# A SwiGLU's second down projection by 2x2 block products with seven products instead of eight

## The chip, the cores and the metric

One core of a Trainium2 chip. The metric is the device time of one execution in microseconds (us). The kernel before: median 1369.47 us of 3 runs (1368.84 to 1370.0).

## The reference, cut to what matters

Two post-norm layers over 512 tokens with 1024 channels. Layer 0 has a convolution and gating mixer, layer 1 dilated attention; after each mixer stands a SwiGLU with 2816 hidden channels, and after each of the four sublayers a LayerNorm.

```python
def swiglu(x, w_gate, w_up, w_down):
    return (jax.nn.silu(x @ w_gate) * (x @ w_up)) @ w_down

for layer in range(DEPTH):                      # DEPTH = 2
    h = ...                                     # mixer
    x = layer_norm(DN_ALPHA * x + h, ln_g[layer, 0], ln_b[layer, 0])
    x = layer_norm(DN_ALPHA * x + swiglu(x, ffn_w_gate[layer], ffn_w_up[layer], ffn_w_down[layer]),
                   ln_g[layer, 1], ln_b[layer, 1])
```

The change touches `@ w_down` of layer 1: hidden values (512 tokens x 2816) times weights (2816 x 1024). All values are float32.

## The kernel before, in words

**Products in three parts.** Each float32 operand is split into a high part (rounded to float32r) and a low part (the rest). A product is three matmuls: high x high, high x low, low x high (`tokens`, L730 to L736). ScalarE makes the high parts (`split_high`, L1191 to L1201), GpSimd the low parts of weights (`split_low`, L615 to L618), VectorE the low parts of activations (`low_ht`, L2028 to L2032).

**Slabs.** Weights stream in slabs of 128 x 1024 floats (512 KB) through a ring of four: four staging buffers, four high and four low. SP loads slab n when the low part of slab n-4 is done (`load_view`, L513 to L524). ScalarE makes the high part of slab n when TensorE has used slab n-4 (`w_used`). Every engine has one instruction queue that runs in the order written; semaphores join them.

**Up projection.** The gate and up products of 20 of the 22 hidden tiles (units) already use a seven-product scheme whose weight sums VectorE makes in SBUF. The last unit's hidden tile is made by `corner_12` (L2014), ScalarE's `unit_gate` (L1445) and `unit_hidden` (L2020, L2025).

**Second down projection.** It is the last stage before the last norm. Row tile k of the hidden values (128 channels x 512 tokens) is multiplied with slab k: four token tiles x two column halves x three matmuls, 24 matmuls of 128x128 by 128x512 (`whole_rows`, L886). The results of all tiles fill the eight PSUM banks, two banks for each token tile. The last three slabs go token tile by token tile (`finish_tiles`, L900), so that the norm of one tile runs while the next is multiplied. For the hidden tiles ScalarE writes the high part (`high_ht`, L1450 to L1457) and VectorE the low part, into nine slots.

**Last norm.** For each token tile: VectorE adds the residual and sums (`norm_in`, L1664, L1668), ScalarE squares and sums (L1221) and takes the root (L1226), VectorE applies the gain (L1684) and takes the reciprocal (L1689), ScalarE scales into `x_res` (L1234, L1237), GpSimd adds the shift (L626). The last tile ends on VectorE instead (L1680, L1693, L1698).

**Attention.** It takes 72 slabs, in two turns of four heads: first queries and keys, then twelve slabs of values. GpSimd does nothing there but the low parts, in a loop of four. At the end of a turn, behind the values' slabs, ScalarE's queue sends row statistics and factors through device memory (`far_rows`, `far_nat`, `fac_rows`, `fac_far`, and the 1 MB `v_rows`), VectorE weighs the probabilities with them (L2191, L2192), and TensorE transposes them (L1080).

## Time and profile before

| | |
|---|---|
| median of 3 runs | 1369.47 us (1368.84 to 1370.0) |
| profiled execution: span | 1369.0 us, 20672 instructions; no time around it is listed |
| TensorE matmul busy | 1355.4 us, 99% |
| VectorE, ScalarE, GpSimd busy | 887.1 us (65%), 615.3 us (45%), 451.1 us (33%) |
| granted TensorE clock, mean | 0.997 of full speed |
| device memory | 133.56 MB read, 4.24 MB written, 101 GB/s over the span |

Busy time of TensorE counts overlapping matmuls once, so 99% says that it is nearly never without one. In a timeline row stand the start, the duration, engine and line, and in brackets the idle time before it and what ended that; "x2" marks merged instructions. The duration of an instruction includes its fill and drain: the next of the same engine can start a little before its end, so two starts tell the pitch. PE is TensorE, PEld its weight loads, DVE VectorE, ACT ScalarE, POOL GpSimd, SP the queue that issues the loads.

### The profile page before, as it was taken

How to read it: one execution, taken by the hardware profiler on the slowest of the kernel's cores; microseconds unless marked ns; L12 is line 12 of the kernel's file. 1: busy time of each engine (PE TensorE's matmuls, PEld its weight loads, DVE VectorE, ACT ScalarE, POOL GpSimd, SP SyncE). 2: the span in 40 equal slices, each digit the busy share in tenths (PEclk: the TensorE clock that was granted, in tenths of full speed). 3: DMA queues.
4: the chain of work that ended last, by engine and by line, in shares of the span. 5: the costliest groups of instructions: out<-in, count | busy, mean ns of one | idle time of the engine just before them, and what ended most of it. 6: DMA issues, size and time to landing. Idle time of an engine off the chain costs nothing.

```text
span 1369.0 us, 20672 instructions
## 1 busy us (share of the span) xinstructions
PE 1355.4 (99%) x8121; PEld 1208.5 (88%) x8121; DVE 887.1 (65%) x1122; ACT 615.3 (45%) x959; POOL 451.1 (33%) x218
## 2 busy tenths in 40 slices
PE   8999999999999999999999999999999999999997
PEld 7887899999988889888888888888889999998886
DVE  3997698888856355677433665724159888885445
ACT  4465555555542454333433434434255555554233
POOL 4785600000054454344443332444260000005443
PEclk9999999999999999999999999999999999999999
DMA  9323223343453323332442322254122334335321
GB/s 269 93 94 92 63 78 108 92 122 92 112 167 95 105 62 93 93 93 84 132 124 67 88 82 73 77 164 130 47 62 78 107 92 122 92 113 164 96 74 62
DMA packets 181961, 138.72 MB, mean 101 GB/s; under 512 B 8789, under 2 KB 162153, under 8 KB 181896
## 3 DMA queue, kind: packets, MB, share of 16 engines
q1 hardware_dynamic: 175272, 133.52, 33.3%
q10 hardware_dynamic: 6624, 4.29, 1.3%
q8 instruction: 45, 0.74, 0.2%
q14 instruction: 20, 0.16, 0.0%
HBM read 133.56 MB, written 4.24 MB: 101 GB/s over the span
## 4 chain that ended last, share of the span: by engine, by line
PE 97%; DVE 1%; DMA 1%; ACT 1%; SPq 0%; issue 0%; DVEq 0%
PE pq L940 10%; PE pq L939 10%; PE pq L937 10%; PE pq L712 9%; PE pq L714 9%; PE pq L713 9%; PE pq L734 8%; PE pq L735 8%; PE pq L736 8%; PE pq L1130 3%; PE pq L1131 3%; PE pq L1129 3%; PE pq L1108 1%; PE pq L1067 1%; PE pq L1080 1%; PE pq L1101 1%
## 5 line engine op out<-in xcount | busy, mean ns | idle before, releaser
L618 POOL TENSOR_TENSOR w_lo<-stage,w_hi 128x1024 fp32r<-128x1024 f32 x154 | 374.5, 2441 | 873.9 <-ACT w_hi L1201 873.8
L1201 ACT ACTIVATE w_hi<-stage 128x1024 fp32r<-128x1024 f32 x156 | 161.6, 1056 | 238.2 <-PE pq L736 164.8
L712 PE MATMUL pq<-xt_hi,w_hi 128*128 128x512 f32 (+1 forms) x624 | 228.4, 366 | 0.5 <-DVE xt_lo L1653 0.4
L714 PE MATMUL pq<-xt_hi,w_lo 128*128 128x512 f32 (+1 forms) x624 | 225.2, 361 | 0.0
L713 PE MATMUL pq<-xt_lo,w_hi 128*128 128x512 f32 (+1 forms) x624 | 225.1, 361 | 0.0
L940 PE MATMUL pq<-xt_hi,w_lo 128*128 128x256 f32 x632 | 178.9, 283 | 0.0
L939 PE MATMUL pq<-xt_lo,w_hi 128*128 128x256 f32 x632 | 178.9, 283 | 0.0
L937 PE MATMUL pq<-xt_hi,w_hi 128*128 128x256 f32 x632 | 178.8, 283 | 0.0
L712 PEld LDWEIGHTS pq<-xt_hi,w_hi 128*128 128x128 f32 x624 | 117.9, 189 | 19.5 <-DVE xt_lo L1653 1.2
L714 PEld LDWEIGHTS pq<-xt_hi,w_lo 128*128 128x128 f32 x624 | 117.8, 189 | 18.0
L937 PE MATMUL pq<-xs_hi,w_hi 128*128 128x256 f32 x472 | 133.6, 283 | 0.0
L939 PE MATMUL pq<-xs_lo,w_hi 128*128 128x256 f32 x472 | 133.6, 283 | 0.0
L940 PE MATMUL pq<-xs_hi,w_lo 128*128 128x256 f32 x472 | 133.6, 283 | 0.0
L713 PEld LDWEIGHTS pq<-xt_lo,w_hi 128*128 128x128 f32 x624 | 117.9, 189 | 17.1
L937 PEld LDWEIGHTS pq<-xt_hi,w_hi 128*128 128x128 f32 x632 | 121.3, 192 | 0.1
L939 PEld LDWEIGHTS pq<-xt_lo,w_hi 128*128 128x128 f32 x632 | 121.3, 192 | 0.1
L940 PEld LDWEIGHTS pq<-xt_hi,w_lo 128*128 128x128 f32 x632 | 121.3, 192 | 0.0
L2032 DVE TENSOR_TENSOR xs_lo<-ht,xs_hi 128x512 fp32r<-128x512 f32 x26 | 63.4, 2440 | 67.7 <-ACT xs_hi L1457 67.7
L937 PEld LDWEIGHTS pq<-xs_hi,w_hi 128*128 128x128 f32 x472 | 90.6, 192 | 0.0
L939 PEld LDWEIGHTS pq<-xs_lo,w_hi 128*128 128x128 f32 x472 | 90.6, 192 | 0.0
L940 PEld LDWEIGHTS pq<-xs_hi,w_lo 128*128 128x128 f32 x472 | 90.6, 192 | 0.0
L734 PE MATMUL pq<-w_hi,xs_hi 128*128 128x512 f32 x208 | 81.0, 389 | 0.0
(261 smaller groups left out, 2808.4 us busy)
## 6 DMA issues: line engine op xcount, KB each, us to landing
stage<-in_od_w_qkv_dram SPq DMA_DIRECT2D x72, 512.0 KB, 3.9
stage<-in_ffn_w_gate_dram SPq DMA_DIRECT2D x44, 512.0 KB, 4.9
stage<-in_ffn_w_up_dram SPq DMA_DIRECT2D x44, 512.0 KB, 3.9
stage<-in_ffn_w_down_dram SPq DMA_DIRECT2D x44, 512.0 KB, 3.5
stage<-in_ev_w_in_dram SPq DMA_DIRECT2D x16, 512.0 KB, 5.7
stage<-in_ev_w_out_dram SPq DMA_DIRECT2D x8, 512.0 KB, 3.6
stage<-in_od_w_out_dram SPq DMA_DIRECT2D x8, 512.0 KB, 3.9
x_res<-in_x_dram SPq DMA_DIRECT2D x4, 512.0 KB, 6.2
```

The lines of the kernel that those rows point to most:

```text
L618: pool.tensor_tensor(w_lo[slab % RING][:, :], w_stage[slab % RING][:, :], w_hi[slab % RING][:, :].bitcast(F32), ALU.subtract).then_inc(w_l ...
L712: pe.matmul(o, hi[:, k, :], x_hi, start=(k == 0), stop=False)
L713: pe.matmul(o, hi[:, k, :], x_lo, start=False, stop=False)
L714: last = pe.matmul(o, lo[:, k, :], x_hi, start=False, stop=(k == KD - 1))
L734: pe.matmul(o, t_hi[:, tile * P:(tile + 1) * P], hi, start=first, stop=False)
L735: pe.matmul(o, t_hi[:, tile * P:(tile + 1) * P], lo, start=False, stop=False)
L736: return pe.matmul(o, t_lo[:, tile * P:(tile + 1) * P], hi, start=False, stop=end)
L937: pe.matmul(o, hi[:, k, :], x_block[0][:, k, :], start=(first and k == 0), stop=False, skip_group_check=True)
L939: pe.matmul(o, hi[:, k, :], x_block[1][:, k, :], start=False, stop=False, skip_group_check=True)
L940: last = pe.matmul(o, lo[:, k, :], x_block[0][:, k, :], start=False, stop=(k == KH - 1), skip_group_check=True)
L1201: act.activation(w_hi[slab % RING][:, :], w_stage[slab % RING][:, :], ACT.Copy).then_inc(w_hi_ready, 1)
L2032: dve.tensor_tensor(lo, ht[:, k, :], hi.bitcast(F32), ALU.subtract).then_inc(ht_set, 1)
```

## The change: what it does, and the diff

The hidden values H are cut into 2 x 2 blocks for each pair of row tiles (two channel tiles x two halves of 256 tokens), the weights W of the pair into 2 x 2 blocks (two row tiles x two halves of 512 columns). With sums of blocks of H and of W, seven block products for each of the 11 pairs give the result instead of eight; a block product is 6 matmuls.

- **Weight sums.** During attention GpSimd issues six steps per pair (`block_sums`), one behind each low part: three copies and four adding transfers, all from device memory to device memory, into `t_rows`, with three waits for landing per pair. Each pair has two slabs of sums (2 x 512 KB) and a half slab; its seven transfers write 2.5 MB. GpSimd's loop over the attention slabs is written out.
- **39 slabs instead of 22**, numbered here 0 to 38: 0 to 21 are the two sum slabs of each pair, 22 and 23 plain rows of the first two pairs, 24 to 29 the fourth sums (29 is half a slab), 30 to 38 plain rows of the other nine pairs. SP waits for all sums before slab 0.
- **Low parts.** GpSimd makes those of slabs 0 to 3, VectorE those of slabs 4 to 38.
- **Hidden sums.** VectorE forms three sums per pair and later a fourth; ScalarE rounds them, VectorE makes their low parts.
- **Corners.** After the eleventh pair ScalarE copies two token-pairs' results out of PSUM and VectorE combines them in four steps; the rows then accumulate onto the banks.
- **Order at the end.** Token tiles 0 and 1 are complete after slab 29, tiles 2 and 3 after slab 38. The norm of tiles 0 and 1 is interleaved, on ScalarE's and VectorE's queues, with slabs 33, 34 and 35 to 38 (`between`).

```diff
...
-N_SLABS = S_DOWN1 + N_DOWN
+PAIRS = KF // 2
+FRONT_ROWS = 2
+SUM4_SLABS = (PAIRS + 1) // 2
+S_REST = S_DOWN1 + 2 * PAIRS
+S_SUM4 = S_REST + FRONT_ROWS
+S_ROWS = S_SUM4 + SUM4_SLABS
+N_SLABS = S_ROWS + PAIRS - FRONT_ROWS
+OP_SLOTS = 4
...
+            if S_DOWN1 <= slab < S_REST:
+                return t_rows[slab - S_DOWN1].unsqueeze(1)
+            if S_SUM4 <= slab < S_ROWS:
+                return t_rows[2 * PAIRS + slab - S_SUM4][:, 0:slab_width(slab)].unsqueeze(1)
+            if slab >= S_REST:
+                return rows(ffn_w_down[1], 2 * row_pair(slab) + 1)
...
+            def load_down(first, layer, e, end):
+                if layer:
+                    sp.wait_ge(t_four, 16 * PAIRS)
                 load(first)
                 load(first + 1)
                 load_ln(e, layer, 1)
-                for slab in range(first + 2, first + N_DOWN):
+                for slab in range(first + 2, end):
                     load(slab)
...
+            def block_sums(j, step):
+                left, right = slice(0, 512), slice(512, SLAB)
+                upper, lower = (ffn_w_down[1][(2 * j + n) * P:(2 * j + n + 1) * P, :] for n in range(2))
+                both, own = t_rows[2 * j], t_rows[2 * j + 1]
+                four = t_rows[2 * PAIRS + j // 2][:, (j % 2) * 512:(j % 2) * 512 + 512]
+                if step == 0:
+                    pool.dma_start(own, upper).then_inc(t_copied, 16)
+                elif step == 1:
+                    pool.dma_start(both.rearrange("p (a n) -> p a n", a=2),
+                                   lower[:, right].unsqueeze(1).broadcast_to([P, 2, 512])).then_inc(t_copied, 16)
+                    pool.dma_start(four, lower[:, left]).then_inc(t_copied, 16)
+                elif step == 2:
+                    pool.wait_ge(t_copied, 48 * (j + 1))
+                    pool.dma_start(both.rearrange("p (a n) -> p a n", a=2),
+                                   upper[:, right].unsqueeze(1).broadcast_to([P, 2, 512]), accum_op=ALU.add
+                                   ).then_inc(t_two, 16)
+                elif step == 3:
+                    pool.dma_start(own[:, right], upper[:, left], accum_op=ALU.add).then_inc(t_two, 16)
+                elif step == 4:
+                    pool.wait_ge(t_two, 32 * (j + 1))
+                    pool.dma_start(both[:, left], upper[:, left], accum_op=ALU.add).then_inc(t_three, 16)
+                else:
+                    pool.wait_ge(t_three, 16 * (j + 1))
+                    pool.dma_start(four, both[:, left], accum_op=ALU.add).then_inc(t_four, 16)
             feed_forward(S_DOWN0, 1)
-            with pool.Fori(0, N_ATT // RING - 1) as t:
-                for j in range(RING):
-                    split_low(S_ATT + RING + j, t)
+            for n, slab in enumerate(range(S_ATT + RING, S_OUT1)):
+                split_low(slab)
+                if n < 6 * PAIRS:
+                    block_sums(*divmod(n, 6))
             for slab in range(S_OUT1, S_UP1):
                 split_low(slab)
             norm(2, S_UP1)
-            feed_forward(S_DOWN1, 3)
+            for slab in range(S_DOWN1, S_DOWN1 + RING):
+                split_low(slab)
+            norm(3, N_SLABS)
...
+            def down_by_blocks(down, done):
+                def product(slab, side, t_hi, t_lo, part, tile, right, first=False, end=False, resumed=False):
...
+                for j in range(PAIRS):
+                    both, own = down + 2 * j, down + 2 * j + 1
+                    op, first, end = op_pair(j), j == 0, j == PAIRS - 1
+                    def by_three(): return product(both, 0, *op, 2, 0, 1, first, end)
+                    def by_two(): return product(both, 1, *op, 0, 0, 0, first, end)
+                    def by_own(): return product(own, 0, *op, 3, 2, 0, first, end)
+                    def by_own_two(): return product(own, 1, *op, 1, 2, 1, first, end)
+                    slab_ready(both)
+                    pe.wait_ge(op_lo_set, 2 * j + 1)
+                    if not end:
+                        by_three()
+                        by_two().then_inc(w_used, 1)
+                        slab_ready(own)
+                        pe.wait_ge(op_lo_set, 2 * j + 2)
+                        if first:
+                            pe.wait_ge(hid_set, done + KF)
+                        by_own()
+                        by_own_two().then_inc(w_used, 1)
+                        continue
+                    slab_ready(own)
+                    pe.wait_ge(op_lo_set, 2 * j + 2)
+                    by_own()
+                    by_three().then_inc(m_done, 1)
+                    by_own_two().then_inc(m_done, 1)
+                    by_two().then_inc(w_used, 2)
...
+                def plain_rows(slab):
+                    rows_ready(slab)
+                    if slab == S_REST:
+                        pe.wait_ge(corner_set, 1)
+                    op = op_row(slab - S_REST)
+                    product(slab, 0, *op, 1, 2, 0, resumed=True)
+                    if slab == S_REST:
+                        pe.wait_ge(corner_set, 2)
+                    product(slab, 1, *op, 0, 2, 1, resumed=True).then_inc(w_used, 1)
+                for slab in range(S_REST, S_SUM4):
+                    plain_rows(slab)
+                pe.wait_ge(corner_set, 4)
+                for slab in range(S_SUM4, S_ROWS):
+                    rows_ready(slab)
...
+                for slab in range(S_ROWS, N_SLABS - 3):
+                    plain_rows(slab)
+                for slab in range(N_SLABS - 3, N_SLABS):
+                    rows_ready(slab)
+                for r in range(2):
+                    for slab in range(N_SLABS - 3, N_SLABS):
+                        t_hi, t_lo = op_row(slab - S_REST)
+                        for side in range(2):
+                            part = slice((1 - side) * HALF, (2 - side) * HALF)
+                            last = tokens(slab, 512 * side, 512, pq[:, 2 * (2 + r) + side, :], t_hi[:, part], t_lo[:, part],
+                                          r, False, slab == N_SLABS - 1, True)
+                        if r:
+                            last.then_inc(w_used, 1)
+                    if r == 0:
+                        last.then_inc(acc_done, 1)
...
+                def high_sums(j):
+                    act.wait_ge(h_sum_set, 2 * j + 2)
...
+                    act.activation(op_pair(j)[0][:, 0:3 * HALF].rearrange("p (b n) -> p b n", n=HALF), pair_sums(j), ACT.Copy
+                                   ).then_inc(op_hi_set, 1)
+                def high_own(j):
+                    act.wait_ge(hid_set, done + 2 * j + 1)
+                    act.activation(op_pair(j)[0][:, 3 * HALF:4 * HALF], pair_blocks(j)[:, 1, :], ACT.Copy
+                                   ).then_inc(op_hi_set, 1)
+                def high_row(slab):
+                    split_high(slab)
...
+                    act.activation(op_row(m)[0][:, 0:src.shape[1] * HALF].rearrange("p (b n) -> p b n", n=HALF), src, ACT.Copy
+                                   ).then_inc(op_hi_set, 1)
...
                 root(0)
+                if between:
+                    between(0)
                 scale(0)
                 squares_of(1)
                 root(1)
+                if between:
+                    between(1)
                 if e == 3:
                     act.wait_ge(x_scaled, SCALED_PARTS * e + 2)
                     act.wait_ge(ln_loaded[e], 32)
                     act.activation(tile_banks(0), halves(norm_g[:, :]), ACT.Copy).then_inc(gain_copied, 1)
                 scale(1)
+                if between:
+                    between(2)
...
+                if layer:
+                    high_sums(0)
+                    split_high(down + 1)
+                    high_own(0)
+                    unit_gate(last, last % 2)
+                    split_high(down + 2)
+                    split_high(down + 3)
+                    high_sums(1)
+                    high_own(1)
+                    for j in range(2, PAIRS):
+                        split_high(down + 2 * j)
+                        split_high(down + 2 * j + 1)
+                        high_sums(j)
+                        high_own(j)
+                    for slab in range(S_REST, S_SUM4):
+                        high_row(slab)
+                    for n, (dst, bank) in enumerate(((sums, 1), (gate, 5))):
+                        act.wait_ge(m_done, n + 1)
+                        for r in range(2):
+                            last = act.activation(dst[:, r, :], pq[:, bank + 2 * r, :], ACT.Copy)
+                        last.then_inc(m_kept_set, 1)
+                    for slab in range(S_SUM4, S_ROWS + 3):
+                        high_row(slab)
+                    def between(n):
+                        for slab in ((S_ROWS + 3,), (S_ROWS + 4,), range(S_ROWS + 5, N_SLABS))[n]:
+                            high_row(slab)
+                    norm(e, N_SLABS, between)
+                    return
...
+                if e == 3 and i == 1:
+                    dve.wait_ge(w_used, plain(S_ROWS))
+                elif i < TILES - 1:
+                    dve.wait_ge(acc_done, e * (TILES - 1) + i + (e < 3 or i == 0))
                 else:
...
+            def norm(e, between=None):
                 def low(i):
                     if e < 3:
                         x_low(e + 1, i)
                 norm_in(e, 0)
+                if between:
+                    between(0)
                 norm_gain(e, 0)
                 norm_scale(e, 0)
                 norm_in(e, 1)
+                if between:
+                    between(1)
                 norm_gain(e, 1)
                 norm_scale(e, 1)
+                if between:
+                    between(2)
...
+                def low_slab(slab):
+                    width = slab_width(slab)
+                    dve.wait_ge(w_hi_ready, plain(slab) + 1)
+                    dve.wait_ge(w_lo_ready, plain(slab))
+                    dve.tensor_tensor(w_lo[slab % RING][:, 0:width], w_stage[slab % RING][:, 0:width],
+                                      w_hi[slab % RING][:, 0:width].bitcast(F32), ALU.subtract).then_inc(w_lo_ready, 1)
+                def sums_of(j):
+                    blocks, room = pair_blocks(j), pair_sums(j)
+                    dve.wait_ge(hid_set, done + 2 * j + 2)
...
+                    dve.tensor_tensor(room[:, 0:2, :], blocks[:, 1:3, :], blocks[:, 0:1, :].broadcast_to([P, 2, HALF]),
+                                      ALU.subtract).then_inc(h_sum_set, 1)
+                    dve.wait_ge(h_sum_set, 2 * j + 1)
+                    dve.tensor_tensor(room[:, 2, :], room[:, 1, :], blocks[:, 1, :], ALU.add).then_inc(h_sum_set, 1)
+                def fourth_sum(j):
+                    blocks, room = pair_blocks(j), pair_sums(j)
+                    dve.wait_ge(h_sum_set, 2 * j + 2)
+                    dve.tensor_tensor(blocks[:, 0, :], blocks[:, 3, :], room[:, 2, :], ALU.subtract).then_inc(h_four_set, 1)
+                def low_sums(j):
+                    hi, lo = (t[:, 0:3 * HALF].rearrange("p (b n) -> p b n", n=HALF) for t in op_pair(j))
+                    dve.wait_ge(op_hi_set, 2 * j + 1)
+                    dve.tensor_tensor(lo, pair_sums(j), hi.bitcast(F32), ALU.subtract).then_inc(op_lo_set, 1)
+                def low_own(j):
+                    hi, lo = (t[:, 3 * HALF:4 * HALF] for t in op_pair(j))
+                    dve.wait_ge(op_hi_set, 2 * j + 2)
+                    dve.tensor_tensor(lo, pair_blocks(j)[:, 1, :], hi.bitcast(F32), ALU.subtract).then_inc(op_lo_set, 1)
+                def low_row(slab):
+                    low_slab(slab)
+                    m = slab - S_REST
+                    src = row_blocks(slab)
+                    hi, lo = (t[:, 0:src.shape[1] * HALF].rearrange("p (b n) -> p b n", n=HALF) for t in op_row(m))
...
+                    dve.wait_ge(op_hi_set, 2 * PAIRS + m + 1)
+                    dve.tensor_tensor(lo, src, hi.bitcast(F32), ALU.subtract).then_inc(op_lo_set, 1)
+                def corners(n):
+                    if n == 0:
+                        dve.wait_ge(m_kept_set, 1)
+                    elif n == 1:
+                        dve.wait_ge(corner_set, 1)
+                        dve.wait_ge(m_kept_set, 2)
+                    elif n == 2:
+                        dve.wait_ge(w_used, plain(S_REST))
+                        dve.wait_ge(corner_set, 1)
+                    else:
+                        dve.wait_ge(corner_set, 3)
+                    for r in range(2):
...
+                    last.then_inc(corner_set, 1)
+                def down_by_blocks():
+                    sums_of(1)
+                    low_own(0)
+                    corner_12(UNITS - 1, (UNITS - 1) % 2)
+                    unit_hidden(UNITS - 1, (UNITS - 1) % 2)
+                    fourth_sum(0)
+                    low_sums(1)
+                    low_own(1)
+                    fourth_sum(1)
+                    sums_of(2)
+                    for j in range(2, PAIRS):
+                        low_slab(S_DOWN1 + 2 * j)
+                        fourth_sum(j)
+                        if j < PAIRS - 1:
+                            sums_of(j + 1)
+                        low_slab(S_DOWN1 + 2 * j + 1)
+                        low_sums(j)
+                        low_own(j)
+                    for slab in range(S_REST, S_SUM4):
+                        low_row(slab)
+                    for n in range(4):
+                        corners(n)
+                    for slab in range(S_SUM4, S_ROWS + 3):
+                        low_row(slab)
+                    def between(n):
+                        for slab in ((S_ROWS + 3,), (S_ROWS + 4,), range(S_ROWS + 5, N_SLABS))[n]:
+                            low_row(slab)
+                    dve.wait_ge(corner_set, 4)
+                    norm(3, between)
...
+                if layer:
+                    sums_of(0)
+                    low_sums(0)
+                    down_by_blocks()
+                    return
...
```

## Rows read from the trace of the kernel before

**Rows 1.** The profile's page: busy time of TensorE, and its most frequent weight load.
```profile
PE 1355.4 (99%) x8121; PEld 1208.5 (88%) x8121; DVE 887.1 (65%) x1122; ACT 615.3 (45%) x959; POOL 451.1 (33%) x218
...
L713 PEld LDWEIGHTS pq<-xt_lo,w_hi 128*128 128x128 f32 x624 | 117.9, 189 | 17.1
```

**Rows 2.** Waits by total: who waited for whom, us, times, longest us.
```profile
POOL w_lo L618 <- ACT w_hi L1201: 873.8, 104, 208.9
...
PE pq L748 <- DMA x_res<-in_x_dram: 3.4, 2, 3.0
```

**Rows 3.** TensorE's timeline, first and last matmul of the second down projection (528).
```profile
1240.61 0.40 PE L734 MATMUL pq<-w_hi,hr_hi 128*128 128x512 f32 x1
...
1360.09 0.39 PE L736 MATMUL pq<-w_hi,xs_lo 128*128 128x512 f32 x1
```

**Rows 4.** Timeline of VectorE, then ScalarE: start us, us, operation [idle before].
```profile
1119.92 0.43 DVE L2012 TENSOR_TENSOR pq<-pq,z_kept 128x256 f32<-128x256 f32 x1 [0.29 <-PE pq L940]
1120.26 1.21 DVE L1976 TENSOR_TENSOR w_lo<-stage,w_hi 128x1024 fp32r<-128x1024 f32 x1
1121.39 0.68 DVE L1988 TENSOR_TENSOR w_lo<-sums,w_hi 128x512 fp32r<-128x512 f32 x1
1122.32 1.23 DVE L1955 TENSOR_TENSOR sums<-stage 128x1024 f32<-128x1024 f32 x1 [0.25 <-DMA stage<-in_ffn_w_up_dram]
1123.65 0.69 DVE L1964 TENSOR_TENSOR sums<-sums,stage 128x512 f32<-128x512 f32 x1
1124.26 0.41 DVE L2017 TENSOR_TENSOR gate<-u_kept,pq 128x256 f32<-128x256 f32 x1
...
1236.26 0.62 ACT L1457 ACTIVATE hr_hi<-ht 128x512 fp32r<-128x512 f32 x1
1236.78 1.99 ACT L1201 ACTIVATE w_hi<-stage 128x1024 fp32r<-128x1024 f32 x2
```

**Rows 5.** Timeline at the entry of the second down projection: VectorE, then GpSimd.
```profile
1238.03 0.69 DVE L2025 TENSOR_TENSOR ht<-pq,gate 128x512 f32<-128x512 f32 x1 [1.03 <-PE pq L940]
...
1241.90 0.69 DVE L2025 TENSOR_TENSOR ht<-pq,gate 128x512 f32<-128x512 f32 x1 [0.70 <-ACT gate L1448]
...
1243.61 2.88 DVE L2032 TENSOR_TENSOR xs_lo<-ht,xs_hi 128x512 fp32r<-128x512 f32 x1
...
1235.54 10.41 POOL L618 TENSOR_TENSOR w_lo<-stage,w_hi 128x1024 fp32r<-128x1024 f32 x4 [208.91 <-ACT w_hi L1201]
1247.47 2.40 POOL L618 TENSOR_TENSOR w_lo<-stage,w_hi 128x1024 fp32r<-128x1024 f32 x1 [1.53 <-ACT w_hi L1201]
```

**Rows 6.** Timeline of the last norm's first tile: VectorE, then ScalarE.
```profile
1348.27 1.23 DVE L1664 SCALAR_TENSOR_TENSOR pq<-x_res,pq 128x1024 f32<-128x1024 f32 x1 [5.37 <-PE pq L736]
...
1351.10 1.29 DVE L1684 SCALAR_TENSOR_TENSOR pq<-pq,neg_mean,norm_g 128x1024 f32<-128x1024 f32 x1 [1.35 <-ACT xt_lo L1221]
...
1349.79 1.12 ACT L1221 ACTIVATE xt_lo<-pq,neg_mean 128x1024 fp32r<-128x1024 f32 x1 [9.39 <-DVE neg_mean L1668]
...
1351.01 1.28 ACT L1226 ACT_TABLE_LOAD   x1
1352.30 0.29 ACT L1226 ACTIVATE std<-sq_sum,eps 128x1 f32<-128x1 f32 x1
```

**Rows 7.** DMA issues (KB, us to landing); second turn's timeline, VectorE and TensorE.
```profile
stage<-in_ffn_w_down_dram SPq DMA_DIRECT2D x44, 512.0 KB, 3.5
...
v_rows<-v_att ACTq DMA_DIRECT2D x2, 1024.0 KB, 6.6
...
921.73 2.42 DVE L2191 TENSOR_SCALAR probs<-probs,m_fac 128x128 f32<-128x128 f32 x1 [11.34 <-DMA fac_far<-fac_rows]
...
928.08 0.27 DVE L2191 TENSOR_SCALAR probs<-probs,m_fac 128x128 f32<-128x128 f32 x1
...
932.47 1.80 PE L1080 MATMUL pq<-ident,probs 128*128 128x128 f32 x15
```

**Rows 8.** Windows, 11 to 16 us: busy us by engine, granted clock, DMA share, GB/s.
```profile
11.00:16.00 5.00, 4.66 (x29) 4.42 (x27) 2.67 (x4) 3.73 (x6) 2.15 (x2) 0.66 1.10 277
```

119 lines of the change are left out of this document (102 added, 17 removed).

## The prediction

> **What bounds the kernel now.** I read the busy shares first: TensorE is busy 99% of the span [rows 1]. The list of waits comes next: TensorE's longest is 3.0 us, at the very start, and none falls in the stage that changes, while GpSimd idles 873.8 us waiting for ScalarE's rounded slabs [rows 2]. So TensorE's instruction stream is the time, and everything else hides behind it. Then the timeline of TensorE in the second down projection: the first matmul starts at 1240.61, the last at 1360.09 [rows 3]. That is 22 slabs x 24 = 528 matmuls and 527 intervals, 119.48 / 527 = 0.2267 us each, gapless: 5.44 us per slab. The profiled execution's own time is its span of 1369.0 us, with nothing listed around it; the median of the runs is 1369.47, 0.5 above and within the runs' scatter, so I add differences to 1369.47.
>
> **Removed.** The same result is made by 7 block products instead of 8. Per pair of row tiles four products of 6 matmuls stay in the pair loop (264 in all), eleven plain row slabs take 12 each (132), the fourth-sum slabs 11 x 6 = 66: 462 matmuls instead of 528. 66 x 0.2267 = **15.0 us less** if TensorE never waits.
>
> **Added beside it.** VectorE takes over 35 of 39 low parts from GpSimd, makes the sums and the corners; ScalarE rounds 39 slabs instead of 22. Prices [rows 4]: VectorE 1024 columns 1.22 us (next start after 1.13), 512 columns 0.69 (0.60), 256 columns 0.43 (0.34), and 0.1 more where it waits for its own result; 768 by interpolation 0.95 (0.87). ScalarE 1.05 (0.95) for 1024, 0.62 (0.52) for 512, 0.84 between them for 768. After a wait TensorE restarts some 0.15 us late, an estimate under the 0.19 of a weight load [rows 1]; the stalls below hold it. I laid these in the order written in the diff, engine by engine, from the times at which the old stage hands over.
>
> *The entry.* [rows 5] show a lock. A VectorE subtraction with both inputs in SBUF of 512 columns takes 2.88 us at 1243.61, while GpSimd splits, and ends at 1246.49, 0.54 us after the fourth split's end (1235.54 + 10.41); the one at 1238.03, which reads PSUM in the same split run, takes its 0.69. The two alternate.
> - VectorE is free at 1238.03 + 0.60. Its two sums of pair 0 end at 1239.8, ScalarE's rounding at 1240.7, the low part at 1241.7. TensorE wants it at 1240.6: 1.2 us.
> - ScalarE splits slab 1 only after that, so GpSimd runs 1242.3 to 1244.7 and VectorE's sums of pair 1 and the own low part stand behind it. Only then come the last unit's corner, its gate (0.63) and its hidden tile, 1247.2. Before, that tile was there at 1242.6 [rows 5]. TensorE, with 12 matmuls (2.7 us) done, has waited since 1244.6: 2.85 us.
> - GpSimd's slab 2 (1247.5 to 1249.9) holds the low sums of pair 1: 0.9 us. Its slab 3 (to 1253.2) holds the own part; behind that VectorE has 0.4 + 0.4 + 1.1 + 1.2 + 0.4 + 1.1 + 1.2 + 0.95 = 6.75 us of work to the low sums of pair 2, at 1260.0, wanted at 1256.5: 3.7 us.
> Entry: **8.7 us** of stall.
>
> *Pairs 3 to 10.* VectorE per pair: two slabs 2.4, sums 1.1, fourth sum 0.4, low sums 0.9, own 0.4 = 5.2 us under TensorE's 5.44. Cost nothing; if each operation is 5% dearer, some 2 us over the stage. ScalarE needs 3.1. The cover is thin but real.
>
> *Corners.* ScalarE's two copies (1.2) and VectorE's two subtractions (1.3) follow the eleventh pair's second block product, against two more, 12 matmuls (2.7): 0.25, and 0.25 where the first fourth-sum slab queues behind the corners. **0.5 us**.
>
> *The rows with the norms between them.* From [rows 6], one tile: sum 1.33 and mean to the square's start 1.52, square with its read 1.24, square root 0.29, and before the first one a table load of 1.28; gain 1.29. The diff puts slab 33 (the fourth of nine last rows) behind the first root on ScalarE; slab 34 behind the second root; slabs 35 to 38 behind the second scale.
> - Slab 33: the first tile starts at 1331.8 after VectorE's backlog, its root is at 1336.1, then split 1.05, low 1.2, operand low 0.7: 1339.1 against 1338.2. With the restart 1.1 us.
> - Slab 34, in series from 1339.0: gain 1.2, sum to square's start 1.6, square 1.3, root 0.2, split 1.05, low 1.2, operand 0.7 = 7.25, so 1346.3; TensorE has finished slab 33 at 1342.0: 4.4 us.
> - Slab 35: gain 1.3, scale 1.25, split 1.05, low 1.2, operand 0.7 = 5.5 us after 1346.1, so 1351.7; TensorE is through at 1349.1: 2.8 us.
> - Slabs 36 to 38 are asked for together: VectorE has three times 1.85 behind 1351.7, so 1357.3; TensorE is through at 1354.6: 2.8 us.
> Sum: **11.1 us**. The last two tiles' norms stand as before, 18 matmuls (4.1 us) apart: the tail behind the last matmul is unchanged.
>
> *Attention.* POOL's queue gets 77 transfers, 2.5 MB a pair and 28 MB in all, three waits per pair, one step behind each slab. Queued behind each wait is the next slab's low part, and TensorE behind that. Nearest rows: 512 KB land in 3.5 us and 1024 KB in 6.6 us [rows 7]; a step has 24 matmuls = 5.4 us before the next. Below: 0, since GpSimd has its idle time. A gain is excluded. Above: each hop of the factors' exchange late by one 3.5 us transfer. In the second turn VectorE waits 11.34 us for the factors, begins at 921.73, has the first head weighed at 928.1, and TensorE reads it at 932.47 [rows 7]: 4.3 us of slack; three hops late would leave 3 x 3.5 - 4.3 = 6 us. I take 0, as the transfers are spread and the slabs are prefetched four deep; 6 stays for the range. The load of the late stage doubles to one 512 KB slab per 2.7 us, 193 GB/s; a landing of 3.5 us against 8 us of lead is covered up to about 6. GpSimd idled 208.91 us before the first split of this stage [rows 5], so SP's new wait for the last sums is met some 200 us early. GpSimd's loop unrolled: nothing.
> The Trainium skill speaks against this part: "Collectives: The Full Stack", The bandwidth ceiling, says that an adding transfer reads two sources where a copy reads one, and runs at about half a copy's rate. By that rule an estimate for 512 KB is at most twice the copy's time; the sum above does not use it, and no row of before has such a transfer.
>
> **Sum.** -15.0 + 8.7 + 0.5 + 11.1 = +5.3; 1369.47 + 5.3 = **1374.8 us**.
>
> **Rivals.**
> 1. *The norms don't hold the rows.* The place is slabs 33 to 38, price 11.1 us: 1374.8 - 11.1 = **1363.7**, faster. For: tiles 0 and 1 are complete with nine row slabs (9 x 2.72 = 24.5 us) to go, and two norms are only some 6 us of VectorE's time and 7 of ScalarE's. Against: both queues run in order. It decides if the split of slab 34 comes before ScalarE's second square. Chance 0.17; with the entry cheap as well, down to 1354.5, which is inside the same case's far end.
> 2. *No lock at the entry.* Without the waits for GpSimd the same walk gives 3.0 instead of 8.7 us: **1369**, no change. Against it [rows 5]. With the other partial covers: 0.2.
> 3. *The clock falls in the new waits.* After TensorE's wait of 3.0 us early on [rows 2] the granted clock of the next 5 us is 0.66 [rows 8]: part of it at the 1.2 GHz level, while TensorE was working again. That is 5 x (1 - 0.66) = 1.7 us lost. Three of my stalls (3.7, 4.4, 2.8) could do that: 3 x 1.7 = 5.1, **1379.9**. Part is absorbed where VectorE is the limit anyway. Chance 0.15. The Trainium skill, "TensorE: Matmul & The Clock Gate", Part 1, has the rule that an idle array falls to 1.2 GHz and returns only after sustained work. By that rule this case occurs; the early stretch agrees.
> 4. *The transfers in attention come late*, by contention with the exchange or because an adding one takes twice a copy's 3.5 us: 1374.8 + 6 = **1381**, open above: 10 us per pair beyond the slack would be 110 us. Chance 0.1.
> 5. *The change doesn't remove what it says*, or its matmuls run at a wider pitch: the count follows from the loops and the shapes are the old ones, so 0.01.
> The forecast itself: 0.37.
>
> **Numbers.** A measurement of this kernel can tell about 0.2%, 2.7 us, from no change. Slower: forecast, 3, 4 = 0.6 and the dearer part of 2; same 0.18; faster 0.2. Range: from 1363, case 1, to 1385, case 4 with case 3; what lies below (full 15 us gain) or above is under 0.2.
>
> **What would show it.** TensorE's matmuls in the second down projection are 462, at 0.227 us pitch; the list of waits gains TensorE waiting for VectorE, some 20 us in about ten waits, at the first three pairs and at slabs 33 to 36, the largest on slab 34 (4.4); ScalarE's second square stands ahead of that slab's split; GpSimd's slab 1 starts near 1242 and the last hidden tile lands near 1247; granted clock 1.0 in the attention stage and no TensorE wait there. Wrong if: TensorE has no wait in the row slabs (case 1), subtractions beside GpSimd take 0.7 us (case 2), the clock shows 0.5 near slab 34 or pair 2 (case 3), or TensorE waits on GpSimd's low parts between 520 and 960 us (case 4).

## The result, and the profile after

The changed kernel takes 1392.29 us (median of 4 runs, 1390.8 to 1392.61) against 1369.74 us (4 runs, 1368.84 to 1370.52) for the kernel before: ratio 1.0164, 95% interval 1.0152 to 1.0176. It is slower by 22.5 us, where 5.3 had been forecast. The profiled execution took 1390.8 us, with a span of 1389.0 against 1369.0 before: 20.0 us to account for.

The page after, busy time and DMA: the first line answers to [rows 1], the transfers' lines to [rows 7] (KB each, median us to landing).
```profile
PE 1351.8 (97%) x8055; PEld 1201.0 (86%) x8055; DVE 952.4 (69%) x1215; ACT 642.0 (46%) x997; POOL 463.1 (33%) x277
...
q0 software_dynamic: 10560, 28.84, 8.8%
...
t_rows<-in_ffn_w_down_dram POOLq DMA_DIRECT2D x33, 512.0 KB, 5.9
...
v_rows<-v_att ACTq DMA_DIRECT2D x2, 1024.0 KB, 9.5
...
far_rows<-st_far ACTq DMA_DIRECT2D x8, 4.0 KB, 3.7
```
The 66 matmuls are gone (8121 to 8055). But 28.84 MB of new transfers run, and those of attention's exchange have become slower beside them: v_rows lands in 9.5 us instead of 6.6, far_rows (4 KB) in 3.7 instead of 1.7, fac_rows (8 KB) in 9.7 instead of 6.4.

TensorE's three largest groups of waits after, which answer to [rows 2]: line, releaser, us, times, longest.
```profile
PE pq L1315 <- ACT v_att L1847: 7.6, 3, 5.0
PE pq L833 <- DVE xs_lo L2349: 7.1, 3, 4.0
PE pq L1266 <- DVE probs L2576: 4.7, 1, 4.7
```
Two of these groups, L1315 and L1266 with 12.2 us, have nothing to do with the second down projection. They are attention's value projection and the turning of its probabilities. TensorE's timeline says where they are (start us, us, [idle before <- releaser]).
```profile
678.80 0.66 PE L1315 MATMUL pq<-w_hi,xt_hi 128*128 128x512 f32 x1 [4.97 <-ACT v_att L1847]
911.70 0.47 PE L1315 MATMUL pq<-w_hi,xt_hi 128*128 128x512 f32 x1 [1.73 <-ACT v_att L1847]
...
945.00 3.30 PE L1266 MATMUL pq<-ident,probs 128*128 128x128 f32 x15 [4.65 <-DVE probs L2576]
1028.54 0.38 PE L811 MATMUL pq<-xt_hi,w_hi 128*128 128x256 f32 x1 [0.17 <-DVE xt_lo L1911]
...
1256.03 0.47 PE L833 MATMUL pq<-w_hi,hr_hi 128*128 128x512 f32 x1 [1.03 <-DVE hr_lo L2332]
1261.22 0.47 PE L833 MATMUL pq<-w_hi,hr_hi 128*128 128x512 f32 x1 [2.22 <-DVE ht L2291]
1273.20 0.47 PE L833 MATMUL pq<-w_hi,xs_hi 128*128 128x512 f32 x1 [1.90 <-DVE xs_lo L2332]
1352.10 0.47 PE L833 MATMUL pq<-w_hi,hr_hi 128*128 128x512 f32 x1 [0.69 <-DVE hr_lo L2349]
1359.11 0.77 PE L833 MATMUL pq<-w_hi,xs_hi 128*128 128x512 f32 x1 [4.00 <-DVE xs_lo L2349]
1365.44 0.48 PE L833 MATMUL pq<-w_hi,xs_hi 128*128 128x512 f32 x1 [0.88 <-DVE xs_lo L2349]
1370.65 0.47 PE L833 MATMUL pq<-w_hi,xs_hi 128*128 128x512 f32 x1 [2.22 <-DVE xs_lo L2349]
```
The marks give the budget. From attention's first projection (504.57 after, 506.88 before) to the second up projection's first matmul (1028.54, before 1014.32) it is 524.0 us against 507.4: **attention has grown by 16.5 us**. The second down projection, from 1255.0 where TensorE first asks for it to its end at 1380.5, takes 125.5 us against 119.7: **+5.8**. All that lies ahead of attention took 2.3 us less in this execution, the up projection 0.2 more, the tail 0.2 less: -2.3 + 16.5 + 0.2 + 5.8 - 0.2 = 20.0. The -2.3 is not the change's: it lies in the first 17 us, where TensorE comes to the same matmul at 14.86 instead of 17.19, because in this execution the input landed earlier and no stretch at half clock followed, as one does in [rows 8]. Without it the parts give 22.3, the 22.5 of the medians.

Windows after (busy us of PE, PEld, DVE, ACT, POOL; granted clock; DMA share; GB/s): behind five of the waits there is a stretch at the 1.2 GHz level.
```profile
675.00:690.00 15.00, 11.20 (x42) 9.14 (x43) 3.26 (x9) 4.29 (x7) 8.95 (x5) 0.89 0.81 203
940.00:955.00 15.00, 10.35 (x47) 8.79 (x46) 12.17 (x33) 3.17 (x4) 3.32 (x2) 0.89 0.34 111
1256.00:1361.00 105.00, 96.16 (x407) 77.59 (x408) 86.23 (x116) 60.84 (x84) 10.71 (x5) 0.97 0.52 167
...
1362.00:1375.00 13.00, 9.91 (x32) 7.07 (x31) 7.95 (x8) 5.45 (x8) 1.61 (x2) 0.76 0.16 66
```
0.89 over 15 us is 1.65 us lost, twice in attention: 12.2 + 3.3 + four restarts of 0.15 = 16.1 of the 16.5. In the second down projection the waits are 12.9 us, and windows of 5 us add up to 6.8 us lost to the clock (somewhat too much, since the clock had fallen before the wait of 4.0 us was over): -15.0 + 12.9 + 6.8 + 7 x 0.15 = +5.8.

**What holds attention.** The first turn's end after, VectorE, then GpSimd:
```profile
665.55 3.90 DVE L2545 TENSOR_SCALAR st_far<-st_far 128x4 f32<-128x4 f32 x1
...
666.22 0.77 POOL L760 DMA_DIRECT2D t_rows<-in_ffn_w_down_dram  x1
666.78 2.63 POOL L687 TENSOR_TENSOR w_lo<-stage,w_hi 128x1024 fp32r<-128x1024 f32 x1
```
Counted from attention's start, VectorE comes to this statistic at the same moment as before, but it takes 3.90 us instead of 0.17: it comes up beside a split with an issue behind it, and ends with the next split (669.41), 3.7 us late. Then ScalarE's queue waits for far_rows to land, and only behind that stands the copy `v_att` that TensorE needs: 6.5 us from the issue (671.60 to 678.06), before 4.3, so 2.2 more. Together 5.9 us, of which 4.97 reach TensorE.

The second turn's end after, ScalarE's queue, VectorE, GpSimd:
```profile
905.06 2.23 ACTq L1863 DMA_DIRECT2D far_rows<-st_far  x4
...
917.32 0.37 ACTq L1873 DMA_DIRECT2D fac_rows<-fac_tok  x1
...
912.48 0.19 DVE L2551 TENSOR_TENSOR m_low<-st_near,far_nat 128x16 f32<-128x16 f32 x1 [9.56 <-DMA far_nat<-far_rows]
...
933.30 2.27 DVE L2575 TENSOR_SCALAR probs<-probs,m_fac 128x128 f32<-128x128 f32 x1 [15.94 <-DMA fac_far<-fac_rows]
935.50 5.64 DVE L2576 TENSOR_SCALAR probs<-probs,fac_far 128x256 f32<-128x256 f32 x1
...
933.11 2.38 POOL L687 TENSOR_TENSOR w_lo<-stage,w_hi 128x1024 fp32r<-128x1024 f32 x1 [6.82 <-ACT w_hi L1388]
935.43 0.80 POOL L777 DMA_DIRECT2D t_rows<-t_rows  x1
936.00 4.98 POOL L687 TENSOR_TENSOR w_lo<-stage,w_hi 128x1024 fp32r<-128x1024 f32 x2
```
Three delays stand in a row. From the issue of far_rows to VectorE's m_low: 7.4 us (905.06 to 912.48), before 4.8. From the issue of fac_rows to the first weighing: 16.0 us (917.32 to 933.30), before 11.4 (910.36 to [rows 7]'s 921.73). The first head's eight weighings: 11.5 us, to 944.78, before 6.35 [rows 7], because two of them are held longer or anew: one of 0.34 us of work takes 5.64 (before 2.50), and a later one 2.49 (before 0.34). The first begins beside GpSimd's issue of a transfer (935.43) and ends 0.16 us after the two splits behind that issue (936.00 + 4.98). 2.6 + 4.6 + 5.1 = 12.3, less the 4.3 of slack that the prediction read: 8.0, against 7.3 us of waits at this turn's end.

### The profile page after: what moved, and what is told of

Same layout as the page of the kernel before. It is cut to its first block, busy times and chain, and to the rows that moved or that the text cites. A ratio compares the mean times of both kernels' runs of the same rounds, so it can differ in the third digit from the quotient of the medians.

```text
span 1389.0 us, 20711 instructions
## 1 busy us (share of the span) xinstructions
PE 1351.8 (97%) x8055; PEld 1201.0 (86%) x8055; DVE 952.4 (69%) x1215; ACT 642.0 (46%) x997; POOL 463.1 (33%) x277
## 3 DMA queue, kind: packets, MB, share of 16 engines
q0 software_dynamic: 10560, 28.84, 8.8%
## 4 chain that ended last, share of the span: by engine, by line
PE 90%; DVE 4%; DMA 2%; ACT 2%; issue 1%; ACTq 0%; SPq 0%; DVEq 0%
PE pq L1122 10%; PE pq L1121 10%; PE pq L1119 10%; PE pq L811 9%; PE pq L812 9%; PE pq L813 9%; PE pq L833 7%; PE pq L835 7%; PE pq L834 7%; PE pq L1315 2%; PE pq L1316 2%; PE pq L1317 2%; PE pq L1266 1%; PE pq L1294 1%; PE pq L1253 1%
## 5 line engine op out<-in xcount | busy, mean ns | idle before, releaser
L687 POOL TENSOR_TENSOR w_lo<-stage,w_hi 128x1024 fp32r<-128x1024 f32 x136 | 336.9, 2482 | 751.0 <-ACT w_hi L1388 750.8
L1388 ACT ACTIVATE w_hi<-stage 128x1024 fp32r<-128x1024 f32 x173 | 179.1, 1053 | 200.1 <-PE pq L835 126.1
L833 PE MATMUL pq<-w_hi,xs_hi 128*128 128x512 f32 x218 | 87.3, 400 | 9.0 <-DVE xs_lo L2349 7.1
L835 PE MATMUL pq<-w_hi,xs_lo 128*128 128x512 f32 x218 | 86.6, 397 | 0.0
```

The lines of the kernel that those rows point to most:

```text
L687: pool.tensor_tensor(w_lo[slab % RING][:, :], w_stage[slab % RING][:, :], w_hi[slab % RING][:, :].bitcast(F32), ALU.subtract).then_inc(w_l ...
L833: pe.matmul(o, t_hi[:, tile * P:(tile + 1) * P], hi, start=first, stop=False, skip_group_check=resumed)
L835: return pe.matmul(o, t_lo[:, tile * P:(tile + 1) * P], hi, start=False, stop=end, skip_group_check=resumed)
L1388: act.activation(w_hi[slab % RING][:, 0:width], w_stage[slab % RING][:, 0:width], ACT.Copy).then_inc(w_hi_ready, 1)
```

## The experiments

Each was run beside the kernel before, whose median was 1368.7 to 1369.2. Times are medians; waits are those of one profiled execution.

**The sums alone.** The kernel before with the 77 transfers, and SyncE's wait for them; nothing reads the sums.
```diff
-            with pool.Fori(0, N_ATT // RING - 1) as t:
-                for j in range(RING):
-                    split_low(S_ATT + RING + j, t)
+            for n, slab in enumerate(range(S_ATT + RING, S_OUT1)):
+                split_low(slab)
+                if n < 6 * PAIRS:
+                    block_sums(*divmod(n, 6))
```


> The kernel before, with only the device-memory sums of the change issued by GpSimd during attention (nothing reads them). The changed kernel's trace puts 16.5 us of its 20.0 us in attention and 5.8 in the second down projection. If the two parts are independent: before + 16 to 20 us (the median of the changed kernel stood 3 us above its profiled span), so 1386 to 1390, with TensorE waiting for the values' copies and for the weighed probabilities at both ends of turns. If the attention loss came only together with the other parts (more slabs, unrolled queue): before + 0 to 3 us.

Measured: 1386.6 us, ratio 1.013 (1.0113 to 1.0147): 17.9 us for a part taken as nothing. TensorE's waits of this kernel:
```profile
PE pq L1166 <- ACT v_att L1626: 6.2, 2, 4.7
PE pq L1117 <- DVE probs L2229: 4.5, 1, 4.5
```
They are the ones of after, with no block product in the kernel.

**No sums.** The changed kernel without them; the sum slabs are loaded from plain rows of w_down, so the sums are left out.
```diff
-                return t_rows[slab - S_DOWN1].unsqueeze(1)
+                return rows(ffn_w_down[1], slab - S_DOWN1)
```


> The changed kernel without the device-memory sums: the sum slabs are loaded from rows of the weights instead, same sizes and number, so the product is not the reference's. If my walk through the second down projection was right: before + 5.3 us (1375), with the waits of TensorE as in the changed kernel's trace and none in attention. If the late stage's stalls come from loads of the sums, it would be near before - 10 us.

Measured: 1375.58 us, ratio 1.0043 (1.0026 to 1.0059), 6.9 us over before by the medians and 5.9 by the ratio; attention has no TensorE wait. Waits of the second down projection in this kernel:
```profile
PE pq L798 <- DVE xs_lo L2314: 7.1, 3, 4.0
PE pq L798 <- DVE xs_lo L2297: 3.3, 2, 2.8
...
PE pq L798 <- DVE ht L2256: 2.2, 1, 2.2
PE pq L798 <- DVE hr_lo L2297: 1.0, 1, 1.0
```
So the excess over the kernel before splits into 17.9 and 6 to 7, together 24 to 25 for 22.5 measured: two nearly independent parts. The forecast of 1374.8, which had attention at 0, is within 0.8 us of this kernel's time (partly by luck, see below). Pair 2's wait is 2.8 here and 1.9 after.

**Sums in the up projections.** Five pairs' steps behind the norm ahead of the first up projection, six behind that of the second, none in attention.
```diff
             norm(0, S_UP0)
+            for j in range(5):
+                for step in range(6):
+                    block_sums(j, step)
```


> The same sums, issued not in attention but in the two up projections, where GpSimd idles 209 us each: five pairs in the first, six in the second. Theory A (the attention's small exchanges through device memory are held up by the bulk transfers) and theory B (GpSimd's queue, held by its waits, delays the low parts) both give about before + 6 (1375) here, plus what the up projection's loads lose: the loads there land in 4.9 and 3.9 us with little slack on VectorE, 0 to 3 us. If a bulk transfer costs wherever it is put, it stays at +16 to +22.

Measured: 1415.49 us, ratio 1.0334 (1.0317 to 1.0351), 46.8 us over before and above every case named. GpSimd is idle in those stages, but their slabs are not ahead of their use: VectorE waits 37.6 us for loads of up projection rows there (before 4.2), TensorE behind it, and the mean granted clock falls to 0.980.
```profile
PE pq L1125 <- DVE ht L2297: 24.6, 9, 4.8
```
An idle engine was the wrong thing to look for; what counts is whether the loads beside the transfers have slack.

**Sums behind the slabs of queries and keys only.** 42 steps in attention, away from the turns' ends; the other 24 in the second up projection.
```diff
-                if n < 6 * PAIRS:
+                if (slab - S_ATT) % TURN_SLABS in range(4, QK_SLABS + 1):
```


> The sums behind the query and key slabs of attention alone, none behind the values' slabs where the turns end; the rest of the steps in the second up projection. Theory A: the loss sits at the ends of turns, so this gives before + 6 to 8 us (1375 to 1378). Theory B: GpSimd's waits and issue cost behind every slab, so half to two thirds of the 16.5 us stays: 1383 or more.

Measured: 1388.65 us (1383.56 to 1391.0), ratio 1.0147 (1.0129 to 1.0165). The time is one that theory B named, the mechanism is theory A's: with 42 of the 66 steps still in it, attention has no TensorE wait any more, so the loss sits at the turns' ends, not in the number of transfers. Waits of 4.68, 1.20 and 1.69 us have come up in the second up projection. The profiled execution, 1383.56, is the fastest of the four, so 5 us of the median are not in it. VectorE's row behind the late load:
```profile
1055.39 1.23 DVE L2226 TENSOR_TENSOR sums<-stage 128x1024 f32<-128x1024 f32 x1 [5.82 <-DMA stage<-in_ffn_w_up_dram]
```

**The steps placed.** One behind each row slab of the first down projection (22), 42 behind queries and keys, the last two behind the output projection's slabs.
```diff
+            for slab in range(S_DOWN0, S_ATT):
+                split_low(slab)
+                one_step()
+            norm(1, S_ATT)
             for slab in range(S_ATT + RING, S_OUT1):
                 split_low(slab)
+                if (slab - S_ATT) % TURN_SLABS in range(4, QK_SLABS + 1):
+                    one_step()
```


> The changed kernel with the same 66 steps behind other slabs: one behind each of the 22 row slabs of the first down projection, the rest behind the slabs of queries and keys of attention only, none behind a slab of values or at a turn's end. Theory A (the transfers cost only where a small transfer or a loaded slab has no slack, that is at the ends of attention's turns, and in the second up projection): no TensorE wait in attention, none in the first down projection, and the time is that of the kernel without sums, 1375.6, give or take 2. Theory B (each adding transfer costs something wherever it stands, by memory traffic): 1385 to 1392 again, with TensorE's waits moved into the first down projection.

Measured: 1382.8 us, ratio 1.0095 (1.0081 to 1.0109). Between the two theories: 7.2 us over the kernel without sums. Attention's ends are clean, and one new wait has come at the entry of the first down projection. TensorE, VectorE and GpSimd there:
```profile
390.40 0.80 PE L845 MATMUL pq<-w_hi,hr_hi 128*128 128x512 f32 x1 [3.44 <-DVE ht L2303]
...
382.08 6.54 DVE L2310 TENSOR_TENSOR hr_lo<-ht,hr_hi 128x512 fp32r<-128x512 f32 x1
...
382.03 2.43 POOL L687 TENSOR_TENSOR w_lo<-stage,w_hi 128x1024 fp32r<-128x1024 f32 x1
...
384.38 0.76 POOL L762 DMA_DIRECT2D t_rows<-in_ffn_w_down_dram  x1
384.97 0.70 POOL L764 DMA_DIRECT2D t_rows<-in_ffn_w_down_dram  x1
385.51 2.55 POOL L687 TENSOR_TENSOR w_lo<-stage,w_hi 128x1024 fp32r<-128x1024 f32 x1
```
The same subtraction took 2.23 us in the kernel before, beside splits without issues. Here it is not let in when the first split ends (384.46), where two issues follow, but when the second is through (388.06), and ends at 388.62. The granted clock is 0.72 from 388 to 400, 3.4 us lost. 3.4 + 3.4, and a wait of 1.0 for a rotary product in attention, are 7.8, for 7.2 by the medians. The profiled execution is the slowest of its five (1385.5) and stands 9.6 us in span over that of the kernel without sums; 1.6 of these lie at the kernel's start.

**The entry in another order**, on top of the placed steps: VectorE takes slabs 1 to 3 from GpSimd, ScalarE splits slab 1 first, the last unit's corner comes ahead of pair 0's low part. The edit reaches further: in all later pairs too, the sums are rounded and their low parts made ahead of the pair's second slab, and the fourth sum comes last.
```diff
-                    high_sums(0)
                     split_high(down + 1)
-                    high_own(0)
+                    high_sums(0)
                     unit_gate(last, last % 2)
+                    high_own(0)
                     split_high(down + 2)
-                    split_high(down + 3)
                     high_sums(1)
+                    split_high(down + 3)
                     high_own(1)
```


> As the run with the steps placed, and the entry of the second down projection in another order: VectorE takes the low parts of slabs 1 to 3 from GpSimd (so that no two engines subtract from SBUF side by side), ScalarE splits slab 1 first, the last unit's corner comes before the low parts of pair 0's sums. The forecast's lock theory: the entry's stalls (6.5 us in the kernel without sums: 1.0, 2.2, 0.6 and 2.8, and a stretch at half clock) shrink to under 2, and the time falls by 5 to 8 us against the run with the steps placed. Rival (VectorE's work itself is the limit at the entry, not the lock): the stalls move to pairs 1 and 2 and the time falls by less than 2 us.

Measured: 1374.73 us, ratio 1.0047 (1.0033 to 1.006), 8.1 less than placed. The four waits (1.0, 2.2, 0.6, 2.8) have become one of 1.5, and the half clock there is gone. How much of it is the lock and how much the order isn't separated, since one edit changes both.

**The rows in another order**, on top of the placed steps: slab 34's split ahead of the first square, 35 to 37 behind the first root and scale, 38 behind the second root, and TensorE's wait for each slab alone.
```diff
-                for slab in range(N_SLABS - 3, N_SLABS):
-                    rows_ready(slab)
                 for r in range(2):
                     for slab in range(N_SLABS - 3, N_SLABS):
+                        if r == 0:
+                            rows_ready(slab)
```


> As the run with the steps placed, with slabs 34 to 38 split further ahead of the norms (slab 34 ahead of the first tile's square, 35 behind the first root, 36 and 37 behind the first scale, 38 behind the second root; the same for their low parts on VectorE), and TensorE waits for the last three slabs one by one. The forecast's theory (the norms hold the rows): the four stalls there (0.7, 4.0, 0.9, 2.3) fall under 1 us together and with them 4 us of half clock, the time falls by 8 to 12 us against the run with the steps placed. Rival (the half clock has another cause): 6 to 8 us, and the clock near slab 34 stays below 1.

Measured: 1370.4 us (1368.25 to 1374.77), ratio 1.0014 (1.0004 to 1.0023), 12.4 less than placed. Of the four waits (0.7, 4.0, 0.9, 2.3) one of 1.4 us is left.

**Both**: the two diffs above together.

> Both reorderings with the steps placed. Theory: the two add, TensorE has under 4 us of waits in the second down projection, and the time is 1369.5 - 15.0 + 1 to 4 = 1355 to 1359, faster than the kernel before by 0.8 to 1 per cent: the whole of what the removed matmuls were worth less a little. Rival (the sums or the doubled rate of loads set a floor of their own): 1362 or more, with TensorE waiting for slabs' low parts in pairs 3 to 10.

Measured: 1364.3 us (1363.56 to 1366.87), ratio 0.9967 (0.9955 to 0.9979): faster than the kernel before. The two together give 18.5, alone 8.1 + 12.4. The expected 1355 to 1359 was missed by what this kernel still pays at the entry of the first down projection, TensorE's wait of 3.4 us and its half clock. By its time it falls in the rival's case, but the rival's sign, waits in pairs 3 to 10, isn't there.

**The first step four slabs later**, on top of both:
```diff
                 split_low(slab)
-                one_step()
+                if slab >= S_DOWN0 + RING:
+                    one_step()
```


> The run with both reorderings, with the first step behind the fifth row slab of the first down projection instead of the first. In the placed runs TensorE waits 3.4 us at that stage's entry, where a subtraction of VectorE takes 6.5 us while GpSimd alternates splits and transfer issues without a gap, and then a stretch at half clock follows. Theory (GpSimd's issuing of transfers keeps VectorE off its SBUF port just as its subtractions do): without issues in those four slabs the subtraction is back at 2 to 3 us, the wait of 3.4 is gone and with it the half clock, and the time is 1364.3 - 5 = 1359, give or take 1.5. Rival (the wait comes from the extra memory traffic at the entry): it moves or stays, 1363 or more.

Measured: **1358.6 us** (1357.24 to 1358.95), ratio 0.9917 (0.9903 to 0.993). The wait of 3.4 us and its half clock are gone, 5.7 us less for four slabs without issues, and the subtraction takes 2.25 us. The run takes away the transfers' traffic at the entry together with their issues: four steps fewer stand in the stage (21 transfers instead of 26), so it doesn't by itself part the two. What speaks for the issues is that the operation that shrank, from 6.54 to 2.25 us, reads and writes SBUF only. TensorE's largest waits in this kernel:
```profile
PE pq L859 <- DMA x_res<-in_x_dram: 3.0, 3, 2.5
PE pq L845 <- DVE hr_lo L2348: 1.5, 1, 1.5
PE pq L845 <- DVE xs_lo L2365: 1.4, 1, 1.4
```

**Plain copies, no waits.** The changed kernel with 77 plain copies of the same sizes in the same places, into rows that nobody reads, and without GpSimd's waits (the sums are left out).
```diff
-                    pool.wait_ge(t_two, 32 * (j + 1))
-                    pool.dma_start(both[:, left], upper[:, left], accum_op=ALU.add).then_inc(t_three, 16)
+                    pool.dma_start(spare[5][:, left], upper[:, left]).then_inc(t_three, 16)
```


> The changed kernel with its 77 transfers in their old places but as plain copies of the same sizes into rows that nobody reads, and without GpSimd's waits for them; the sum slabs are loaded from plain rows, so the sums are left out. It tells what in the transfers delays the small exchanges at the turns' ends. Theory (the adding transfers' traffic is in the way of the exchange): v_rows lands in 6 to 7 us and far_rows in about 2, TensorE's waits at the turns' ends are mostly gone, 1376 to 1380. Rival 1 (any bulk transfer on GpSimd's queue does it): v_rows 9 and far_rows 3.5 as with the sums, 1388 to 1392. Rival 2 (GpSimd's waits, which make its slabs late): TensorE's waits gone although v_rows still takes 9.

Measured: 1386.81 us, ratio 1.0129 (1.0113 to 1.0144), 5.5 less than the changed kernel and 11.2 more than without sums. Neither clean: attention takes 516.6 us here, 507.4 before, 524.0 after, so by these executions bulk transfers on GpSimd's queue as such cost 9.2 of the 16.5 us, and adding and waiting the other 7.3. v_rows lands in 7.2 us, far_rows in 3.2. At the first turn's end TensorE doesn't wait: there the statistic takes its 0.17 us and far_rows lands in 2.0. At the second turn's end the late weighing is there in full (VectorE, GpSimd of this kernel):
```profile
928.47 5.38 DVE L2569 TENSOR_SCALAR probs<-probs,fac_far 128x256 f32<-128x256 f32 x1
...
928.40 0.52 POOL L770 DMA_DIRECT2D t_rows<-in_ffn_w_down_dram  x1
928.93 4.75 POOL L685 TENSOR_TENSOR w_lo<-stage,w_hi 128x1024 fp32r<-128x1024 f32 x2
```

**Copies by SyncE.** As the one that starts later, with the 33 copies on SyncE's queue, one ahead of a slab's load, and 44 adding transfers on GpSimd's. From the third pair on SyncE also waits for earlier sums before it copies.
```diff
+                if slab < S_ATT + QK_SLABS:
+                    copy_one()
                 load(slab)
```


> As the run that starts later, with the 33 plain copies issued on SyncE's queue ahead of its loads and only the 44 adding transfers on GpSimd's, so that GpSimd issues 44 instead of 77. Theory (GpSimd's issues hold VectorE): VectorE's rotary product in attention, 2.89 us before and 3.7 us with 77 issues, falls to about 3.3 us, and the time is the same as in the run that starts later or up to 2 us less, since little of VectorE's time is on the path. Rival (SyncE's copies stand ahead of its loads in the queue and make slabs late): TensorE or VectorE waits for slabs and the time is 3 us more or worse.

Measured: 1370.5 us, ratio 1.0009 (1.0 to 1.0018): the rival. TensorE waits 7.8 us for rotated queries and keys. The rotary product falls to 3.40 us as expected (2.89 before, 3.56 after, 3.65 with 77 placed issues). But slabs come late and in bunches, GpSimd's splits with them, and the product is held again: here it ends 1.1 us after the second of two splits (566.19), and 1.2 us is all it takes where nothing holds it. ScalarE and VectorE of this kernel:
```profile
554.23 1.06 ACT L1420 ACTIVATE w_hi<-stage 128x1024 fp32r<-128x1024 f32 x1 [3.96 <-DMA stage<-in_od_w_qkv_dram]
...
560.26 7.01 DVE L2554 TENSOR_TENSOR qk<-qk,norm_g 32x1024 f32<-32x1024 f32 x1
```

**Reordered, no sums.** Both reorderings, with the diff of the kernel without sums (the sums are left out).

> Both reorderings without the sums (the sum slabs are loaded from plain rows; the sums are left out): the floor that the block products can reach in this order. Theory: 1375.6 less what the reorderings gave together (1382.8 - 1364.3 = 18.5), so 1357, give or take 1.5, with under 4 us of TensorE waits in the second down projection and none elsewhere. Rival (the two costs overlap, and the transfers hide part): 1360 or more.

Measured: 1357.52 us (1357.2 to 1358.93), ratio 0.9915 (0.9901 to 0.9928). That is the floor in this order. The placed sums stand 1.1 us above it, no more than the scatter of the runs of either: the adding transfers can be had for next to nothing.

## Why the prediction was off, point by point

The direction was right, the size not: +22.5 us against +5.3, and 1392.3 is above the range's upper end of 1385. TensorE's new waits in the second down projection are 12.9 us in seven, where some 20 in about ten were forecast.

- **Removed**: right. 8121 - 8055 = 66 matmuls, and the last ones still start 0.23 us apart.
- **The entry**, 8.7: measured 1.03 + 2.22 + 1.90 = 5.2, with three restarts and the 1.7 us of half clock behind the second one 7.3. The walk held to within 0.8 us. With the stage's start shifted by 14.4 us, GpSimd's slab 1 began at 1241.5 (said: 1242.3) and the hidden tile landed at 1246.7 (1247.2). Pair 1's 0.9 did not come, and pair 2 was overpriced, 3.7 for 1.9. The lock is there: VectorE's sum of 256 columns at 1256.52, beside GpSimd's slab 1, took 2.50 us instead of 0.43.
- **Pairs 3 to 10**, 0, and **the corners**, 0.5: no wait between 1273.20 and 1352.10, so 0 for both.
- **The rows with the norms between them**, 11.1: measured 0.69 (said 1.1), 4.00 (4.4), 0.88 (2.8), 2.22 (2.8), so 7.8, and 5.1 us of half clock in this stretch. The order is the one predicted, ScalarE's second square and root ahead of slab 34's split (after):
```profile
1354.62 1.11 ACT L1409 ACTIVATE xt_lo<-pq,neg_mean 128x1024 fp32r<-128x1024 f32 x1
...
1355.86 0.29 ACT L1414 ACTIVATE std<-sq_sum,eps 128x1 f32<-128x1 f32 x1
1356.06 1.04 ACT L1388 ACTIVATE w_hi<-stage 128x1024 fp32r<-128x1024 f32 x1
```
Slab 35's wait is small because TensorE came to it late itself, at half clock. Rival 1, that the norms don't hold the rows, is out; the run with the rows reordered gave back 12.4 us. Rival 2 is out too.
- **Rival 3**, the clock falls in the new waits, came true beside the forecast: 6.8 us in this stage, 5.1 forecast. The rule of the Trainium skill, "TensorE: Matmul & The Clock Gate", Part 1, that an idle array falls to 1.2 GHz, agrees with these rows. As a term of its own it should have been in the sum and not among the rivals; that the sum fitted without it (+5.3; measured +5.8 in the profile, 6 to 7 alone) is luck: the waits were overpriced by about as much.
- **Attention**, taken as 0 with a bound of 6: **this is the step that failed.** Measured 16.5 in the profile, 17.9 alone. The prediction gave as reason that "the transfers are spread and the slabs are prefetched four deep". The slabs were on time indeed; but the exchange at the end of a turn is not prefetched. It is a chain of small transfers with VectorE and ScalarE waiting for each, with 4.3 us of slack at the second turn's end and about 1 at the first. The bound named this chain but went wrong three times. It took one plain copy's 3.5 us for each hop as the most, where the hop behind v_rows grew by 4.6. It looked at the second turn only, while the first turn's end lost 5.0 us too, on another path: ScalarE's copy of the values behind far_rows. And it left out that the lock read in [rows 5] works on VectorE in attention also: 3.7 us on the first turn's statistic, 5.1 on the second turn's weighing; the lock was known, and was applied only to the stage that the change is about. The clock's fall, 3.3 us, comes on top.
- **Rival 4**, these transfers late, had the right place with a chance of 0.1 and 6 us; its sign, TensorE waiting for GpSimd's low parts, didn't show. The rule beside it, from "Collectives: The Full Stack" of the Trainium skill, The bandwidth ceiling (an adding transfer at about half a copy's rate), is stated there for rings of a collective, and agrees in part. The 5.9 us of the page after mixes 22 copies with 11 adding transfers. By line, the adding transfer of 512 KB (L767) lands in 7.3 us at the median and the plain copy that stands in its place in the run with plain copies in 5.5: 1.3 times, not twice. Loads of 512 KB into SBUF landed in 3.5, so much of the dearness is not in the adding.

What stays open: how much of attention's loss is the transfers' traffic and how much VectorE held by GpSimd. The single rows put 2.2 us of the first turn's chain and 7.2 of the second's on transfers, 3.7 and 5.1 on the hold. No run takes one of the two away alone: with plain copies and no waits, both are gone at the first turn's end.

## What to carry to other kernels

Background transfers cost little by their bytes; they cost where they stand. Put them beside work whose loads have slack, and away from chains of small transfers and from handovers between stages: the same 77 transfers cost 17.9 us in one place and about 1, within the scatter, in another. When work is added to an engine whose instructions hold up another's, apply that hold to every stage in which the new work runs, and list every chain that has less slack than one such hold. A wait of TensorE costs more than its length where the clock falls behind it (1.65 us on top of the waits of 4.97 and 4.65); put that in the sum.

## What the runs showed of the hardware

- An operation of VectorE on SBUF that came up while GpSimd issued a transfer, or beside a split with issues right behind it, was held through the next one or two splits: 6.54 us for 0.69 (placed steps), 5.64 for 0.34 and 3.90 for 0.17 (after), 5.38 for 0.34 (plain copies), 7.01 for a product that takes 2.89 on average before. Beside splits without issues such operations took 2.2 to 2.9 us. That the issue is to blame is read from these rows; the 5.7 us that four slabs without issues gave back agree, though their traffic was gone too. Whether it holds the port itself or only lets the next split in ahead isn't settled; the rotary product in some rows ran on while an issue went on.
- A transfer of 4 KB took twice as long, 1.7 to 3.7 us at the median, beside bulk transfers in another engine's queue (207 and 194 GB/s over the two stretches, 671 to 678 and 905 to 911; before 88 and 85).
- In the changed kernel the clock fell to its lower level behind the waits of 5.0, 4.7 and 4.0 us and behind both of 2.2, each of which stood 5 us behind one of 0.9 to 1.0; behind those of 1.7 and 1.9 us it did not.
